# Hybrid encoder step: feed-forward norm and expert routing rebuilt, prompt tiles routed ahead of the sample tile

## What is computed

```
x = x + cross_attn(rmsnorm(x, g_cross), mem_k, mem_v, w_cq, w_co)
h = rmsnorm(x, g_ffn)
grp_prob = softmax(h @ w_grp + b_grp)              # 4 groups, the best one is taken
e_logits = (h @ w_rt + b_rt)                       # 32 experts, 8 to a group
e_top, e_idx = top_k(e_logits of the best group, 2)
e_w = softmax(e_top) * g_top
x = x + sum of 2 experts: e_w * ((silu(h @ w_gate[e]) * (h @ w_up[e])) @ w_down[e])
y = rmsnorm(x, g_final)
```

## Time and profile before

| | us |
|---|---|
| median of 3 runs | 1346.47 (1344.55 to 1349.22) |
| profiled execution | 1343.79 |
| its span | 1341.9 |
| busy: PE, DVE, ACT, POOL | 1122.7, 429.5, 278.4, 209.1 |

### The profile page before, as it was taken

One profiled execution on the slowest core, in us unless ns is written; L12 is line 12 of the kernel. 1 busy time (PEld: TensorE's weight loads), 2 busy tenths in 40 slices (PEclk: granted clock), 3 DMA queues, 4 the chain that ended last, 5 costly groups with the idle time before them and its releaser, 6 DMA issues.

```text
span 1341.9 us, 15255 instructions
## 1 busy us (share of the span) xinstructions
PE 1122.7 (84%) x6014; PEld 679.4 (51%) x6014; DVE 429.5 (32%) x900; ACT 278.4 (21%) x577; POOL 209.1 (16%) x226
## 2 busy tenths in 40 slices
PE   5999999996878778999799988699758887877770
PEld 3544555543767666666354558344434444444430
DVE  2001233333664756434431013133643111111115
ACT  2000366634331323210200002122101111101101
POOL 1000355501010100100200000000612222222214
PEclk9999999997998989999899998799968999889985
DMA  8211013102113221500745200653376999999966
GB/s 262 64 63 62 3 63 141 63 0 68 63 64 102 69 80 63 157 0 0 236 164 173 99 0 1 251 188 126 140 315 218 418 416 416 416 416 416 416 243 243
DMA packets 86202, 224.71 MB, mean 167 GB/s; under 512 B 19147, under 2 KB 28235, under 8 KB 77310
## 3 DMA queue, kind: packets, MB, share of 16 engines
q1 hardware_dynamic: 78340, 197.49, 39.4%
q0 software_dynamic: 7760, 26.22, 5.0%
q10 hardware_dynamic: 42, 0.17, 0.1%
HBM read 202.46 MB, written 21.40 MB: 167 GB/s over the span
## 4 chain that ended last, share of the span: by engine, by line
PE 54%; issue 17%; DMA 16%; DVE 7%; POOL 2%; SPq 2%; ACT 2%; DVEq 0%; POOLq 0%; ACTq 0%
PE bank L416 17%; PE bank L412 15%; DMA sb_act_a<-w_up 14%; PE bank L2158 4%; PE bank L1075 3%; PE bank L2173 2%; PE bank L1615 1%; PE bank L1685 1%; SPq L2092 1%; DMA sb_W<-cache_mem_v 1%; DVE sb_scr L337 1%; PE bank L722 1%; PE bank L1080 1%; PE bank L742 1%; PE bank L1827 1%
## 5 line engine op out<-in xcount | busy, mean ns | idle before, releaser
L416 PE MATMUL bank<-sb_W,sb_act_a 128*128 128x512 f32 x480 | 219.0, 603 | 1.7 <-issue 1.0
L412 PE MATMUL bank<-sb_act_a,sb_W 128*128 128x512 f32 (+1 forms) x768 | 213.1, 435 | 1.3 <-DVE sb_act_a L344 1.3
L412 PEld LDWEIGHTS bank<-sb_act_a,sb_W 128*128 128x128 f32 x768 | 115.9, 191 | 92.8 <-issue 90.8
L416 PEld LDWEIGHTS bank<-sb_W,sb_act_a 128*128 128x128 f32 x480 | 88.8, 193 | 101.3 <-issue 99.6
L2158 PE MATMUL bank<-sb_W,sb_act_b 128*64 128x256 f32 x512 | 69.0, 430 | 27.3 <-DMA sb_W<-w_up 23.6
L1075 PE MATMUL bank<-sb_x 128*128 128x128 f32 x512 | 68.3, 284 | 9.7 <-DVE sb_x L1464 6.2
L1075 PEld LDWEIGHTS bank<-sb_x 128*128 128x128 f32 x512 | 61.9, 195 | 16.3 <-DVE sb_x L1464 6.5
L2158 PEld LDWEIGHTS bank<-sb_W,sb_act_b 128*64 128x64 f32 x512 | 45.5, 155 | 46.5 <-issue 34.7
L2228 DVE TENSOR_TENSOR sb_act_b<-bank,sb_act_b 128x128 f32<-128x128 f32 x34 | 9.9, 292 | 181.6 <-ACT sb_act_b L2209 181.6
L2130 POOL DMA_INDIRECT pair_rows<-sb_act_b,sb_attn x32 | 31.6, 987 | 210.7 <-DVE sb_act_b L2240 210.7
L2209 ACT ACTIVATE sb_act_b<-bank 128x128 f32<-128x128 f32 x34 | 9.4, 278 | 246.9 <-PE bank L2158 246.9
(11 more groups left out here) (401 smaller groups left out, 1591.3 us busy)
## 6 DMA issues: line engine op xcount, KB each, us to landing
sb_W<-w_gate SPq DMA_DIRECT2D x16, 1024.0 KB, 23.3
sb_W<-w_up SPq DMA_DIRECT2D x16, 1024.0 KB, 25.6
sb_W<-w_down SPq DMA_DIRECT2D x16, 1024.0 KB, 21.4
sb_W<-w_in SPq DMA_DIRECT2D x7, 2048.0 KB, 8.5
sb_conv<-w_gate SPq DMA_DIRECT2D x9, 1024.0 KB, 23.3
sb_conv<-w_up SPq DMA_DIRECT2D x9, 1024.0 KB, 26.1
sb_gz<-w_down SPq DMA_DIRECT2D x9, 1024.0 KB, 22.6
sb_act_a<-w_gate SPq DMA_DIRECT2D x9, 1024.0 KB, 24.1
```

What stands on the lines that cost most here:

```text
L412: mm = nc.tensor.matmul(out[:, 0:cols.stop - cols.start], slot(unit)[:, c, m * P:(m + 1) * P], src[:, c, cols], start=c == 0, stop=c == KC ...
L416: mm = nc.tensor.matmul(out[:, :], src[:, c, ja * P:(ja + 1) * P], w, start=c == 0, stop=c == KC - 1)
```

## The change

The norm no longer scales rows ahead of turning. `x` is turned as it is (`ffn_turn_pe`, `ffn_turn_dve`), for tiles 0 to 2 behind the stream jobs 5 to 7, tile 3 inside job 8, tile 4 behind job 9. The reciprocal root multiplies the logits instead, when they are back in row form. POOL multiplies `x` itself by the gain row, and ACT scales that by the reciprocal root (`ffn_row_act`) before it is stored. The prompt's logits are two column groups of 64 weight columns (36 and zeros), between chunks of job 8; they are turned back in job 9, and DVE picks experts for the prompt ahead of adding job 9, with `max` and `max_index`. Counts and table are made for the prompt first and for the sample tile behind it. Gate and up of experts 0 and 1 are loaded when the last stream is done, their down weights behind job 8, expert 2 behind job 9, expert 3 behind the sample's logits. The tables of extra blocks, the gate weights (with ACT's two Exp) and `route_more_pe` move in among experts 1 to 5. `e_dve` and `r_dve` are armed at the start of `route_prompt_dve`.

```diff
         n_dve: for "ffn" only ev{t}a ev{t}b are left (xn{t} goes)
...
+        def ffn_row_act(act, t):
+            act.wait_ge(n_pool["ffn"][f"rn{t}"], n_pool["ffn"].after(0, f"rn{t}"))
+            act.wait_ge(n_pool["ffn"][f"g{t}"], n_pool["ffn"].after(0, f"g{t}"))
+            nc.scalar.activation(h_row[:, t % 2, :], h_row[:, t % 2, :], ACT.Copy,
+                                 scale=rstd["ffn"][:, t:t + 1]).then_inc(n_act["ffn"].step(f"h{t}"), 1)
...
+        def ffn_turn_pe(pe, t):
...
+            n = ORDER.index(("co", t, 1))
+            pe.wait_ge(taken(n), taken_count(n))
+            for i, ab in enumerate("ab"):
+                if t:
+                    pe.wait_ge(n_dve["ffn"][f"ev{t - 1}{ab}"], n_dve["ffn"].after(0, f"ev{t - 1}{ab}"))
+                for c in range(4):
+                    q = 4 * i + c
+                    mm = nc.tensor.transpose(quarters(bank[4 + i])[:, c, :], x[:, t, q * P:(q + 1) * P], ident)
+                mm.then_inc(s.step(f"tr{t}{ab}"), 1)
...
+        def logits_prompt_pe(pe):
...
+            for c in range(KC):
+                for b in range(2):
+                    mm = nc.tensor.matmul(bank[1][64 * b:64 * b + 64, 0:2 * P], w_route[:, c, :], act_a[:, c, 2 * P * b:2 * P * b + 2 * P],
+                                          start=c == 0, stop=c == KC - 1, skip_group_check=True)
             mm.then_inc(r_pe.step("lgp"), 1)
+
+        def logits_prompt_turn_pe(pe):
+            pe.wait_ge(r_act["lgp"], r_act.after(0, "lgp"))
...
+        def count_prompt_pe(pe):
+            pe.wait_ge(r_dve["px3"], r_dve.after(0, "px3"))
...
+        def first_table(pe, i, start, stop):
+            for b in range(2):
+                mm = nc.tensor.matmul(bank[7][CAP * b:CAP * b + CAP, 0:2 * NE], at_place[:, i, :],
+                                      first_in[:, i, :, :].rearrange("p a n -> p (a n)"), start=start, stop=stop, skip_group_check=True)
+            return mm
...
+        def route_pick_dve(dve, z, T, n):
...
+            for t in tiles:
+                ins = nc.vector.max(top[:, t, :], ml[:, t, :])
...
+            for t in tiles:
+                ins = nc.vector.max_index(top_at[:, t, :], top[:, t, :], ml[:, t, :])
...
+        def route_prompt_dve(dve):
+            tt = nc.vector.tensor_tensor
+            r_dve.arm(dve)
+            e_dve.arm(dve)
...
+            dve.wait_ge(r_pe["ltp"], r_pe.after(0, "ltp"))
+            dve.wait_ge(n_pool["ffn"][f"rn{NTP - 1}"], n_pool["ffn"].after(0, f"rn{NTP - 1}"))
...
         ffn_rows_pool:
+            for t in range(NT):
...
+                if t >= 2:
+                    pool.wait_ge(s_rows[t % 2], 16 * (t // 2))
+                pool.wait_ge(taken(n), taken_count(n))
+                nc.gpsimd.tensor_tensor(h_row[:, t % 2, :].rearrange("q (c p) -> q c p", c=KC), by_chunk(x[:, t, :]),
+                                        by_chunk(gffn_row), ALU.mult).then_inc(s.step(f"g{t}"), 1)
+                norm_pool_tile(pool, "ffn", t, False)
+                pool.wait_ge(n_act["ffn"][f"h{t}"], n_act["ffn"].after(0, f"h{t}"))
+                pool.dma_start(h_rows[t * P:(t + 1) * P, :], h_row[:, t % 2, :]).then_inc(s_rows[t % 2], 16)
...
         moe_sync:
+            sp.wait_ge(xs_pe["pv"], xs_pe.after(NB - 1, "pv"))
+            for e in range(2):
+                load_gu(e, e, None)
+            sp.wait_ge(s_job, CO_JOBS[-2] + 1)
+            for e in range(2):
+                load_down(e, e, None)
             sp.wait_ge(s_job, CO_JOBS[-1] + 1)
+            load(2, 2, None)
+            sp.wait_ge(r_pe["lgs"], r_pe.after(0, "lgs"))
+            load(3, 3, None)
...
         moe_pe, moe_dve, moe_act:
-                if j == 0:
+                if j == 4:
                     route_more_pe(pe)
...
-                if j == 0:
+                if j == 1:
+                    route_blocks_dve(dve)
+                elif j == 2:
+                    route_rounds_dve(dve)
+                elif j == 3:
+                    route_places_dve(dve)
+                elif j == 4:
+                    route_weights_dve(dve)
+                elif j == 5:
                     route_more_dve(dve)
...
+                if j == 2:
+                    route_late_act(act)
...
         PE:
+                if i < NB:
+                    run_jobs(pe, ("co",), act_a, between, [n])
+                    if i >= 5:
+                        ffn_turn_pe(pe, i - 5)
+            first, last = CO_JOBS[NB:]
+            run_jobs(pe, ("co",), act_a, None, [first], range(0, 2))
+            ffn_turn_pe(pe, NTP - 1)
+            run_jobs(pe, ("co",), act_a, None, [first], range(2, 6))
+            logits_prompt_pe(pe)
+            run_jobs(pe, ("co",), act_a, None, [first], range(6, 8))
+            run_jobs(pe, ("co",), act_a, None, [last], range(0, 1))
+            logits_prompt_turn_pe(pe)
+            run_jobs(pe, ("co",), act_a, None, [last], range(1, 8))
+            count_prompt_pe(pe)
+            ffn_turn_pe(pe, NT - 1)
             route_pe(pe)
...
         ACT, behind the last stage of stream b, and then:
+                    if b > 5:
+                        ffn_row_act(act, b - 6)
                     norm_act_tile(act, "ffn", b - 5, x_tile(b - 5), taken(n), taken_count(n))
             for t in (3, 4):
                 n = x_sum("co", t)
+                ffn_row_act(act, t - 1)
+                if t == 4:
+                    route_prompt_act(act)
                 norm_act_tile(act, "ffn", t, x_tile(t), taken(n), taken_count(n))
             route_act(act)
+            ffn_row_act(act, NT - 1)
...
         DVE:
+                if i == NB + 1:
+                    route_prompt_dve(dve)
                 take_jobs("dve", dve, ("co",), rest_dst, None, [n])
+                if i >= 5 and i < NB:
+                    ffn_turn_dve(dve, i - 5)
                 if i == NB - 1:
...
+                    ffn_turn_dve(dve, NTP - 1)
...
         POOL, ahead of the memory norm:
+            nc.gpsimd.memset(w_route[:, :, 36:64], 0.0).then_inc(s_pad, 1)
```

More of the change, by code:

```diff
@@ L1805, in build_encoder_step @@
         e_pe = steps("moe_pe", "tr | gu | ht | d")
-        r_pe = steps("route_pe", "lgp lgs lg cum first more")
+        r_pe = steps("route_pe", "lgp ltp cump lgs lts firstp cums first more")
         r_act = steps("route_act", "lgp lgs ge ee")
         r_dve = steps("route_dve",
[L1809 to L1812, removed]
+                      "lgm lgp gmaxp gsp gqp gidxp mskp mlp mxp ixp ohp Ap px0 px1 px2 px3 fip dselp selp app "
+                      "lgs gmaxs gss gqs gidxs msks mls mxs ixs ohs As pxs fis dsels sels aps cnt token e0 pf pair "
+                      "dm capq nmore one ends cmp more min tab "
+                      "cmp2 nr tabn starts base do osel low os slot off im0 im off2 place mi "
+                      "ge4 gsum w0 w1a w1 w2 token2 e2 pf2 pair2")
+        s_pad = sem("route_weights_padded")
         s_route = sem("route_weights_loaded")
@@ new lines, in step, with after, over, row @@
+            def step(name):
+                return r_dve.step(name + z), 1
+            def after(name):
+                dve.wait_ge(r_dve[name + z], r_dve.after(0, name + z))
+            def over(v, m):
+                return v[:, T].unsqueeze(2).to_broadcast([P, n, m])
+            def row(v, m):
+                return v.unsqueeze(1).to_broadcast([P, n, m])
+            gl, el = lg[:, T, 0:4], lg[:, T, 4:36]
+            after("lg")
+            red(gmax[:, T], gl, AX.X, ALU.max).then_inc(*step("gmax"))
@@ new lines, in route_pick_dve @@
+            after("gmax")
+            tt(g_s[:, T, :], gl, over(gmax, 4), ALU.subtract).then_inc(*step("gs"))
+            after("gs")
+            stt(g_q[:, T, :], g_s[:, T, :], 0.0, row(C("group_less"), 4), ALU.is_equal, ALU.mult).then_inc(*step("gq"))
+            after("gq")
+            red(gidx[:, T], g_q[:, T, :], AX.X, ALU.min).then_inc(*step("gidx"))
+            after("gidx")
+            tt(msk[:, T, :], row(C("group_of"), NE), over(gidx, NE), ALU.not_equal).then_inc(*step("msk"))
@@ L2222, in moe_dve @@
         def moe_dve(dve):
-            e_dve.arm(dve)
             def hidden(j, k):
@@ L2578, in _ @@
             gdn_pool(pool)
+            pool.wait_ge(staged["tile"], staged.after(NTP, "tile"))
+            nc.gpsimd.memset(w_route[:, :, 36:64], 0.0).then_inc(s_pad, 1)
             for k in ("mem", "cross"):
```

338 lines of the change are left out of this document (169 added, 169 removed).

## The result

The changed kernel took 1329.0 us (median of 4 runs, 1326.0 to 1331.9) against 1347.7 in the same session: ratio 0.9864, interval 0.9832 to 0.9896. That is 18.7 us faster, inside the range, but 5.4 less than the 24.1 of the sum: the size of rival (b), one collision, though more than one thing made it up, as the traces show. The profiled execution took 1330.6 us, its span is 1328.8.

A forecast was written before the change was run, and what follows sets the result against it. The full DMA queue of expert weights was taken to bound the kernel, its end following `gate_up(0)` and `down(0)`. 20.0 + 3.05 - 1.1 + 2.2 = 24.1 us off 1346.5 gave 1322.4, range 1316 to 1333.

The forecast's parts named there:

- the sum: Whole kernel: 20.0 at the gathers + 3.05 - 1.1 + 2.2 = 24.1 us gained, giving 1322.4.
- rival (b): Whole kernel: one collision, of port or clock, takes 3.2 to 6 off; gain 17 to 21, some 1327; chance 20%.
- What binds: Expert stretch: DMA is full at 416 GB/s; the 313 us behind `gate_up(0)` and `down(0)` move with their start.
- a window under 390 GB/s between 1010 and 1050 us: Profile after: a sign that experts 1 to 5 pace the queue instead, which would make the forecast wrong.
- Streams: Stream jobs: two raw tiles turned on PE, 0.95 each, put the last stream job's end at 947.9, from 945.99.
- the collision of L1735 with `g1`: Stream job 7: if `g1` starts first, DVE's query copy is held to 941.4 and the whole chain comes 3.2 late.
- The row chain of POOL and ACT: Around the last streams: multiply, root, scaling and store take 6.9 a tile, so `h3` ends at 962.3.
- Job 9: PE waits 1.5 for the logits copy and ends at 969.3; a gap of 2.5 may cost 1.5 more.
- Prompt routing on DVE: After the logits turn: 22 instructions, 6.2, then two `first_in`, 0.8; job 9 added by 970.9.
- Sample tile: After job 9: row store issued 977.2, landed 7.2 later, 984.4; table 983.4; gathers at 984.5, 20.0 earlier.
- `gate_up(0)` and the arming: First expert: the 3.05 wait goes, start 23.0 earlier; `gate_up(0)` takes 7.3 rather than 6.22, minus 1.1.
- What moved into the experts, and the earlier loads: Experts 1 to 5: moved work costs nothing; earlier loads alone gain nothing, but matter now, keeping 12 MiB off the gathers.

The follow-up runs named there:

- copy first: Changed kernel with DVE's copy of the next stream's queries put ahead of the raw tile's evictions: 1326.0 us, ratio 0.9855.
- three edits: Changed kernel with the query copy ahead of the evictions, ACT's logits copy ahead of `h3`, and a row buffer for each prompt tile: 1320.7 us, ratio 0.9792.
- all four: Changed kernel with query copy and logits copy moved ahead, a row buffer per prompt tile, and expert 3's weights behind the first gather: 1318.9 us, ratio 0.9796.
- expert 3 late: Changed kernel with expert 3's weights issued only when the first gather of rows has landed: 1330.7 us, ratio 0.9868.
- loads late: Changed kernel with first weights loaded as before the change: experts 0 to 2 at job 9's end, expert 3 behind the sample's logits: 1329.6 us, ratio 0.9880.
- four buffers: Changed kernel with a row buffer for each prompt tile, rows 2 and 3 in `scr`, the fourth slot's load behind their stores: 1324.4 us, ratio 0.9829.
- the arming alone: Kernel before with only `e_dve.arm(dve)` moved from the start of `moe_dve` to the start of `route_dve`: 1343.7 us against 1347.0, ratio 0.9977.
- the early loads alone: Kernel before with only gate and up of experts 0 and 1 loaded in job 8, their down weights behind it: 1345.0 us, ratio 0.9984.

## Why the prediction was right, and where it was off

**What binds.** Right in the main. The end follows the moment from which DMA is full. The MB moved by W + 200 say it in another way: each MB more than in the kernel after is 2.4 us, and 29.7, 32.5 and 33.8 MB (copy first, three edits, all four) give 2.6, 9.4 and 12.5 us; the last `gate_up` came 3.0, 9.6 and 12.7 sooner. The start of `gate_up(0)`, 3.2, 9.3 and 13.7 sooner, does nearly as well. The two part where a load is held back: expert 3 late has 2.4 us by the MB, 3.8 by the start, and came 0.6 sooner. From before to after they give 15.1 and 14.2, and 18.0 came. I had also named a window under 390 GB/s between 1010 and 1050 us as a sign that the first experts pace the queue. There is one, 310 from 1010 to 1015 us and 200 from 1015 to 1020, but it lies around the first down refill at 1017.06, which is late by the 7.8 us below; from 1020 on it is 418, 393, 422. So behind the first refill the experts don't set the pace.

**Streams and the held copy: the step that failed.** I put the collision of L1735 with `g1` among the things that can spoil it, at +3.2, and left it out of the sum although my own times set the two 0.2 us apart. It happened in every trace that keeps the order, 0.15 to 0.16 apart, and cost 4.3: job 7 with its turned tile took 16.67 us, job 6 before it 12.37, and the last stream job ended at W + 113.3, not W + 108.8. 2.4 are PE's gap, nearly all the rest is the low clock behind it. The edit that moves the copy shows the cause. The Trainium skill has the rule in a sharper form than the one I weighed: in "SBUF — State Buffer", SBUF: two separate sides, the pair of ports that DVE and GpSimd share is "an exclusive lock", and whichever starts first keeps it for its whole instruction; on VectorE's side it names instructions in a two-port mode, among them an fp32 copy within SBUF, and those with two SBUF inputs. By that rule the short instruction waits for the long one to end, and the trace agrees: the copy ended at 945.70, `g1` at 945.61.

**The row chain of POOL and ACT.** 6.9 a tile was right: `g2` to `g3` is 6.94 apart where nothing waits (955.36 to 962.30, loads late). What I missed is the buffer. I looked for the early loads' cost at the sample tile only; but tile 1's store, issued 2.9 us behind them, landed after 10.04 us, and `g3` needs its buffer: +2.5. Loads late and four buffers take it away, each by another way, and both have job 9 added 3.7 to 3.8 us sooner.

**Job 9.** My 1.5 of gap was right where the buffer wait is gone (1.53, 14 matmuls in 6.17). With 2.5 more it was 3.9, and the low clock cost 1.7 on top (I had named 1.5 for that case).

**Prompt routing on DVE.** Mis-sized, in my favour: with `first_in` it took 5.8 (974.44 to 980.2), not 7.0; `max` and the index search cost 0.12 and 0.16 a tile. So PE's job 9, which ended at 982.06, set the moment of adding, not DVE: W + 138.7, against W + 131.8 forecast; the 7 between are the late `h3` and the low clock.

**Sample tile.** From the start of `g4` to the issue of its store went 6.6, forecast were 6.3. The store took 8.4, not 7.2: +1.2. Rows set the gather, as forecast, by 3.7 us: `first` of the prompt took 1.15 us for its 32, not 4.8, so the table was ready at 994.3.

**`gate_up(0)` and the arming.** The arming was right: the 3.05 are gone, and alone they are worth 3.3. `gate_up(0)` itself was priced too high: it took 5.96, not 7.3.

**What moved into the experts, and the earlier loads.** What moved cost nothing, as forecast. Tables, places and `route_more` lie under matmuls, and ACT went to Exp and back in 2.9 us (two table loads of 1.28, at 1022.11 and 1023.74, close together with the instructions around them). The drain of 1.38 a switch that I quoted from the Trainium skill ("ScalarE: Activation LUTs", What ACT_TABLE_LOAD costs) does not show as idle time here. The earlier loads show no gain in either kernel. Before, they had landed anyway, as I had said. After, I had said that they matter, and missed that they also cost: 3.9 us at a row store, against 4.2 saved at the gather (3.56 instead of 7.74).

**The sum.** At the refill of the first down weights 16.3 us were won rather than 24.1. The 7.8 between, along the path: `h1` ended 3.7 later from W than forecast (held copy, with its low clock), the buffer 2.5, the low clock in job 9 1.6, the store 1.2, and some tenths each at `g4`, at the gather's issue and in the round of `gate_up(1)`, 1.0 together; less 0.8 for DVE's pass and 1.3 for `gate_up(0)`. That is 7.9. From there to the last `gate_up` 1.7 came back (264.0 us against 265.8; 263.6 to 264.5 in all other traces of the changed code but that of expert 3 late, with 266.7, and 264.1 with the arming alone; the early loads alone keep 265.8). I can't place that last piece.

So the range held partly by luck. Rival (b) was one collision; what came was a held copy, a buffer wait, the low clock twice and a slower store, 10.0 with the tenths, set against 2.1 that I had priced too high and 1.7 that I hadn't forecast.

## What to carry to other kernels

Where a full transfer queue sets the end, count the bytes moved up to the moment from which every version is full, beside the start of the first consumer. Here the two agreed for edits that shorten the chain, and parted for the edit that started the consumer 3.8 us sooner by holding a load back: only 1.0 MB more had been moved, 2.4 us, and even that wasn't all kept at the end. A collision whose two times lie 0.2 us apart in your own schedule belongs in the sum, with a chance, not in a list of spoilers; moving the short instruction ahead of the long one, a few lines, won 3 us in the trace. And when transfers are moved earlier, look at every buffer whose release is a transfer, not only at the one on the path before.

## What the runs showed of the hardware

- A 0.22 us copy within SBUF on DVE took 3.81 to 3.84 us in six traces where a POOL multiply had started 0.15 to 0.16 us ahead of it, and 0.22 when it came first. DVE instructions that read a PSUM bank kept their time beside such a multiply (L1846 at 959.76 us, 1.29 for two, under the multiply of tile 2). A 512-column compare with two SBUF inputs took 1.75 beside one and ended 0.5 us behind it; before, 1280 columns took 1.49 with POOL idle (L1957).
- In job 9 a PE gap of 0 or 1.5 us left the next 14 matmuls at 6.17 us; gaps of 3.9 and 3.8 made them 7.87 and 8.53, with a granted clock of 0.57 and 0.50 in their first 4 us.
- A 512 KB row store landed after 10.0 us beside 4 MiB of loads issued 3 us ahead of it, though the loads were on another engine's queue, and after 3.0 us with none of them in flight (loads late).
- Executions with the same code ahead of W reached it up to 5.7 us apart, which is nearly a third of the whole gain. Without a common mark two traces of this kernel say little on a few microseconds.
